# Norm: the spreading product right behind the sum, modulation chunks behind it, and other spin counts on TensorE

## What is computed

```python
mod_x = jnp.split((cond_x @ w_mod[l] + b_mod[l])[:, None, :], 6, axis=-1)
hx = modulate(rmsnorm(x, g_norm1[l]), mod_x[0], mod_x[1])
px = split_cols(hx @ w_in[l])
m_x, m_c = mlstm_mixer(px[0:5], pc[0:5], b_gates[l], g_mlstm[l], not last)
d_x, d_c = diff_attention(px[5], px[6], px[7], pc[5], pc[6], pc[7], lam, lam_init, g_subln[l], not last)
c_x = conv_mixer(px[8], w_dw[l], b_dw[l], g_conv_ln[l], b_conv_ln[l])
x = x + mod_x[2] * (jnp.concatenate([m_x, d_x, c_x], axis=-1) @ w_out[l])
x = x + mod_x[5] * ffn(modulate(rmsnorm(x, g_norm2[l]), mod_x[3], mod_x[4]))
```

## Time and profile before

| | |
|---|---|
| median of 3 runs | 1466.93 us (1465.52 to 1468.47) |
| the profiled execution | 1464.65 us, its span 1462.9 us |
| mean granted TensorE clock over the span | 0.973 |
| busy | PE 1395.8 us (95%), PEld 1144.4 (78%), DVE 982.7 (67%), ACT 632.6 (43%), POOL 181.1 (12%) |
| DMA | 267.07 MB, mean 183 GB/s |
| chain that ended last | PE 84%, DVE 8%, issue 3%, ACT 3%, DMA 2% |

### The profile page before, as it was taken

The page is one execution under the profiler, slowest core; times in us unless marked ns, Lnnn a source line. Parts: engine busy times, 40 slices in busy tenths (PEclk is TensorE's granted clock), DMA queues, the critical chain, the costliest instruction groups (busy, mean ns, idle before and its releaser), DMA issues.

```text
span 1462.9 us, 20612 instructions
## 1 busy us (share of the span) xinstructions
PE 1395.8 (95%) x7756; PEld 1144.4 (78%) x7756; DVE 982.7 (67%) x1476; ACT 632.6 (43%) x997; POOL 181.1 (12%) x134
## 2 busy tenths in 40 slices
PE   7999999989999999999999999898999999999996
PEld 4778787567688888888869887687888888888885
DVE  3755876755744344354469685656898998998896
ACT  3434334652310110010035434635677777777774
POOL 0039970000000000000003960000000000000000
PEclk8999999989999999999999999998999999999998
DMA  9254443322323222222233223149977977977940
GB/s 396 103 201 173 173 173 115 124 108 87 144 91 110 87 103 99 79 109 89 112 116 144 87 87 116 58 150 426 380 289 310 346 305 302 356 291 307 355 171 29
DMA packets 30881, 267.07 MB, mean 183 GB/s; under 512 B 3424, under 2 KB 3552, under 8 KB 4960
## 3 DMA queue, kind: packets, MB, share of 16 engines
q1 hardware_dynamic: 30816, 266.16, 47.7%
HBM read 265.09 MB, written 1.05 MB: 182 GB/s over the span
## 4 chain that ended last, share of the span: by engine, by line
PE 84%; DVE 8%; issue 3%; ACT 3%; DMA 2%; SPq 0%; DVEq 0%; ACTq 0%
PE ps L535 38%; PE ps L989 17%; PE ps L1009 7%; PE ps L852 3%; PE ps L557 3%; PE ps L716 2%; PE ps L752 1%; PE ps L681 1%; PE ps L771 1%; PE ps L542 1%; DMA sb_arena<-mod 1%; DVE sb_egu_lo L2007 1%; PE ps L584 1%; DVE sb_h_lo L1540 1%; PE ps L762 1%
## 5 line engine op out<-in xcount | busy, mean ns | idle before, releaser
L535 PE MATMUL ps<-sb_h_hi,sb_w_hi 128*128 128x512 f32 (+1 forms) x640 | 241.9, 378 | 3.0 <-DVE sb_w_lo L1540 2.7
L535 PE MATMUL ps<-sb_h_hi,sb_w_lo 128*128 128x512 f32 (+1 forms) x640 | 239.5, 374 | 0.0
L535 PE MATMUL ps<-sb_h_lo,sb_w_hi 128*128 128x512 f32 (+1 forms) x640 | 239.4, 374 | 0.0
L989 PE MATMUL ps<-sb_egu_lo,sb_h_lo 128*128 128x512 f32 (+1 forms) x384 | 145.2, 378 | 0.0
L535 PEld LDWEIGHTS ps<-sb_h_hi,sb_w_hi 128*128 128x128 f32 x640 | 121.1, 189 | 28.9 <-DVE sb_w_lo L1540 3.6
L535 PEld LDWEIGHTS ps<-sb_h_hi,sb_w_lo 128*128 128x128 f32 x640 | 121.0, 189 | 21.5
L535 PEld LDWEIGHTS ps<-sb_h_lo,sb_w_hi 128*128 128x128 f32 x640 | 121.2, 189 | 20.7
L1539 DVE CAST sb_w_hi<-sb_arena 128x2048 fp32r<-128x2048 f32 (+1 forms) x38 | 45.5, 1197 | 126.0 <-PE ps L535 114.7
L2007 DVE TENSOR_TENSOR sb_egu_lo<-sb_arena,sb_con_r 128x1024 fp32r<-128x1024 f32 x98 | 115.2, 1216 | 15.3 <-ACT sb_con_r L1360 15.1
L2018 DVE TENSOR_TENSOR sb_ew_lo<-sb_arena,sb_ew_hi 128x1024 fp32r<-128x1024 f32 x88 | 107.1, 1216 | 11.5 <-ACT sb_ew_hi L1373 11.5
L2152 POOL TENSOR_SCALAR sb_arena<-sb_arena,sb_small 128x512 f32<-128x512 f32 (+1 forms) x60 | 104.8, 1746 | 5.9
(11 more groups left out here) (325 smaller groups left out, 3037.2 us busy)
## 6 DMA issues: line engine op xcount, KB each, us to landing
sb_arena<-experts SPq DMA_DIRECT2D x90, 1536.0 KB, 8.8
sb_arena<-mod SPq DMA_DIRECT2D x48, 1024.0 KB, 4.9
sb_arena<-in SPq DMA_DIRECT2D x24, 1024.0 KB, 4.8
sb_arena<-gate SPq DMA_DIRECT2D x11, 1024.0 KB, 4.8
sb_arena<-up SPq DMA_DIRECT2D x11, 1024.0 KB, 4.7
sb_arena<-out SPq DMA_DIRECT2D x8, 1024.0 KB, 6.1
sb_arena<-down SPq DMA_DIRECT2D x8, 1024.0 KB, 4.8
sb_arena<-down SPq DMA_DIRECT2D x4, 768.0 KB, 4.1
```

What stands on the lines that cost most here:

```text
L535: ins = pe.matmul(o, left[a], right[b], start=(k == first and n == 0), stop=(k == final and n == len(PRODUCTS) - 1))
L989: ins = pe.matmul(o, x[:, k, :], w[:, span, :], start=(k == 0 and n == 0), stop=(k == KD - 1 and n == 2))
```

## The change

1. `norm_spread` is called at once behind `norm`'s sum, and the whole batch of modulation chunks stands behind it. The argument `between` goes.
2. `norm_spread` opens its PSUM bank first, puts 3 spins ahead of its wait for "ndiag" (not at norm (0, 0)), and then waits.
3. `conv_variance` puts 6 spins (layer 0) or 5 (layer 1) ahead of its wait for the squares.
4. Ahead of the sum of norm (1, 0) stand 7 spins instead of 2; ahead of the experts 12 instead of 5.
5. At the opening norm (0, 0) stands behind the third chunk instead of the fourth and its spread behind the fourth; `SPIN_FIRST` has other counts; ScalarE takes the norm's root ahead of its copy of the modulation row.

```diff
-NORM_AFTER = 3
+NORM_AFTER = 2
...
-SPIN = {("squares", 0, 0): 0, ("squares", 0, 1): 2, ("squares", 1, 0): 2, ("squares", 1, 1): 0,
+SPIN = {("squares", 0, 0): 0, ("squares", 0, 1): 2, ("squares", 1, 0): 7, ("squares", 1, 1): 0,
         ("norm", 0, 0): 5, ("norm", 0, 1): 4, ("norm", 1, 0): 4, ("norm", 1, 1): 1,
         ("heads", 0): 0, ("heads", 1): 5, ("scores", 0): 5, ("scores", 1): 0, ("conv", 0): 0, ("conv", 1): 0,
-        "router": 8, "moe": 5}
+        ("variance", 0): 6, ("variance", 1): 5, "spread": 3, "router": 8, "moe": 12}
...
-SPIN_FIRST = (8, 1, 1, 0, 1, 5, 2, 0)
+SPIN_FIRST = (8, 2, 0, 2, 1, 4, 2, 0)
...
-            def modulation(l, first, between=None):
+            def modulation(l, first):
...
-                    if i == first and between:
-                        between()
...
                 if (l, which) in MOD_NORM:
-                    modulation(1, MOD_NORM[l, which], lambda: norm_spread(l, which))
+                    norm_spread(l, which)
+                    modulation(1, MOD_NORM[l, which])
 
             def norm_spread(l, which):
 
                 lo = low(l) if which else 0
+                o = open_bank(("nscale", l, which))
+                if l + which:
+                    spin(o, SPIN["spread"])
                 pe.wait_ge(*dve_done.at(("ndiag", l, which)))
-                o = open_bank(("nscale", l, which))
...
             def conv_variance(l):
                 lo = low(l)
+                o = open_bank(("cvar", l))
+                spin(o, SPIN["variance", l])
                 pe.wait_ge(*act_done.at(("csq", l)))
-                o = open_bank(("cvar", l))
...
             squared(0, 0)
+            deviation(0, 0)
             modulation_rows(0, 0)
-            deviation(0, 0)
             lead(("in", 0, IN_ORDER[0]))
```

## The result

The changed kernel took 1457.18 us in the median (1456.98 to 1458.52, 4 runs), the kernel before 1466.22 beside it (1465.41 to 1468.47, 4 runs). The ratio is 0.9938, 95% interval 0.9921 to 0.9955: 9.0 us less. The forecast was 1463.0 with a range down to 1459.1, so it is outside the range, on the fast side.

What follows compares the result with a forecast made beforehand. TensorE, 84% of the chain of waits, was taken as the bound, partly at half clock. Terms summed to 3.9 us saved: 1460.8 against the profiled 1464.65, 1463.0 for the median, the runs' median being 2.3 higher; range 1459.1 to 1468.0.

Steps and rivals of the forecast that it cites:

- Opening, +2.4: Opening: TensorE catches up with its data, so the last modulation chunk starts at 35.1, not 37.52; 2.4 us saved.
- Rival 2: Opening: TensorE stays behind its data, the last chunk still starts near 37.5; 1465.4 us, chance 0.12.
- Norm (0, 1), +0.3: Norm (0, 1): three spins behind the sum; 0.7 us saved if the clock holds, 1.2 lost if it falls; 0.3 booked.
- rival 1: At the sums: the clock holds in front of a sum and falls behind it; 0.9 us saved, 1466.0, chance 0.27.
- Norm (1, 0), +0.6: Norm (1, 0): earlier spread; 1.0 us saved with the clock held, 0.6 lost if it falls; 0.6 saved booked.
- Attention 0, +0.9: Opening of attention, layer 0: six spins fill idle time; 1.9 us saved if the clock holds, otherwise 0; half booked.
- Attention 1, +2.7: Opening of attention, layer 1: the sum and "heads" spins run at full clock, ending at 908.3 instead of 911.0; 2.7 us saved.
- Norm (1, 1), -1.1: Norm (1, 1): spins fill the wait, so one chunk more stands ahead of the router; 1.1 us lost.
- Experts, -1.9: Experts: seven more spins exceed TensorE's 1.11 us wait, so the gather starts late; 1.9 us lost.
- rival 3: Spins run at half clock before ready work, the experts' gather starts 6.9 us late; slower, 1470.4 us, chance 0.06.
- Six stretches: Stretches at 0.50 to 0.51 clock at or near edited places: opening, both attention openings, norms (0, 1), (1, 0), experts' start.
- "same": Whole kernel: outcome within 0.2%, about 2.9 us, which a measurement can't tell from no change; chance 0.37.

Runs made afterwards that it cites:

- the norms alone: The kernel before with only the norms' part: spread behind the sum, 3 spins in it, chunks behind, 7 spins ahead of norm (1, 0)'s sum; 1463.0 ± 0.7 us.
- 5 spins at the experts with the projection's: The changed kernel with 5 spins in layer 1's projection wait at 844 and 5 instead of 12 ahead of the experts; 1455.2 ± 0.4 us.
- the best kernel: The changed kernel with 5 spins in the projection's wait, 5 at the experts, norm (1, 1) as before, 5 ahead of the last scatter; 1452.9 ± 0.8 us.

## Why the prediction was wrong

- **Opening, +2.4:** 1.9 in the profile, 1.8 ± 0.75 and 1.7 ± 0.8 in means. The mechanism and its sign (last chunk at 35.1) were right; half clock in the last chunk (1.56 us instead of 1.07) took the rest. Rival 2 is out.
- **Norm (0, 1), +0.3:** -0.4. The clock fell behind the sum with spins on both sides of it, and the spread took 2.08. This is rival 1 at this place, in this execution. With the same spins the clock held here in three other profiles (the norms alone, 5 spins at the experts with the projection's, the first of the best kernel), and the place gained 0.5 in each where 0.7 was booked for that case. The Trainium skill ("TensorE: Matmul & The Clock Gate", HAM oscillation in Part 1) puts falls down to gaps without matmuls, by which spins that fill every wait would prevent them. Here TensorE still waited 0.89 us ahead of the sum, and the clock fell 3.1 us after the sum began, so this trace doesn't decide about that rule. The result is that the spins laid in sometimes weren't enough.
- **Norm (1, 0), +0.6:** +1.8. The clock held. From the sum to the first product it is 9.38 us now and was 11.12. Three chunks and the turned rows took 3.4, where I had 3.8, and of the 1.4 us that my own end (754.5) allowed I booked 0.6, as if the fall were still likely.
- **Attention 0, +0.9:** -0.5. The sum moved and then the wait of 1.39 us let the clock fall all the same; the spread took 2.05 as before. That too was a draw: in the changed kernel without its opening, the wait of 1.39 us was there and the clock held. The spread took 1.10, as it did in the second profile of the best kernel, and the place gained 2.2 us in both where the forecast's upper value was 1.9.

```profile
257.08 1.10 PE L832 MATMUL ps<-sb_rows_n,sb_con 128*128 128x512 f32 x2 [1.39 <-ACT sb_arena L1280]
```

- **Attention 1, +2.7:** +2.8 in the profile, as worked out, and no profile with these spins has half clock there (14 of 14). The mean with them alone gained only 0.8 ± 0.7, so its worth in means stays open.
- **Norm (1, 1), -1.1:** -0.8. **Experts, -1.9:** -1.6 in the profile, -2.1 ± 0.6 in means. The 12 spins ran at full clock (5.43), so rival 3 is out.

The edited places sum to 3.2 where 3.9 was forecast, with errors that cancel, so that closeness is in part luck. What failed lies elsewhere, in two steps:

1. **"The forecast is for the median: 1463.0."** I hung the sum on a median of three runs, 1466.93, and took its distance from the profiled execution as an offset of the kernel. The mean of 107 executions is 1464.35, below even the profiled one. That is 2.6 of the 4.6 us between the forecast and the changed kernel's mean. With it the range's lower end would have been 1456.5. The first comparison's median lay another 1.2 below that mean, by the draw.
2. **"Six stretches ... that lie at or near an edited place."** I left the stretch at 849 in layer 1's projection, and the end of attention, out of the sum since nobody edited them. A fall at a wait that nobody edited can still come or go: 3.1 us in the profiles, and 3.1 ± 1.1 against 0.2 ± 0.8 when the wait is filled in each kernel. It is enough for the other 2.0, which the means leave uncertain by 0.6; that it is all of them is argued, not shown.

The "same" chance of 0.37 rested on rivals 1 and 2, neither of which decided.

## What to carry to other kernels

Where the clock is a resource, a single profile is one draw. What happens at an edited place can be a draw as well, so one profile doesn't give a term its sign. List every stretch at half clock with the wait ahead of it, edited or not, and give each a price and a chance; compare kernels by means of ten executions or more. Spins belong only in waits, and no more than fit: 5 in a wait of 2.4 us freed 3.1 ± 1.1 us in one kernel and 0.2 ± 0.8 in another, 5 one step away from it cost 5, and 7 too many ahead of the gather cost about 2.

## What the runs showed of the hardware

One program's time follows its mean granted clock closely: executions of the kernel before with 0.971 took 1470.2 us, those with 0.979 took 1458.6. The clock of a wait's follow-up isn't fixed by the program: the same 2.36 us wait with the same work around it was followed by half clock in one execution and by full clock in another. And a delay of 2.2 us some 23 us ahead of such a wait, with no edit in between, was followed by 10 us at half clock behind it, in both kernels that had it, where both profiles of the kernel without it had none.

Some places are surer than others. At attention 1 the fall came in 4 of 4 profiles without the spins and in 0 of 14 with them; in the projection's wait in 0 of 7 with them. At norm (1, 0) it came in 5 of 5 with the old order, in 2 of 13 with the new one, and then for 3.4 us instead of 6.8 or 10.2. At norm (0, 1) it came in 5 of 5 with the old order and still in 10 of 13 with the new one.
